# Differential attention: scores kept in SBUF by the maximum's pass, one exponential per map, values in two column tiles

## What is computed

```python
def one_block(qs):                     # a block of 128 queries, all heads
    a, b = qs
    p1 = softmax(einsum('bqhd,bkhd->bhqk', a, k1) * scale)
    p2 = softmax(einsum('bqhd,bkhd->bhqk', b, k2) * scale)
    return einsum('bhqk,bkhd->bqhd', p1 - lam * p2, v)
```

## Time and profile before

| | us |
|---|---|
| median of 3 runs (2815.12 to 2818.55) | 2816.46 |
| span of the profiled execution, first to last instruction | 2814.8 |
| PE busy in the span | 2441.5 (87%) |
| DVE busy | 2020.7 (72%) |
| ACT busy | 1417.5 (50%) |
| POOL busy | 760.7 (27%) |
| differential attention, about 475 to 818 us of the span | 343 |
| the exponential of 1024 scores, L588, 128 times | 143.5 |
| the maximum, L628, 128 times | 155.8 |

### The profile page before, as it was taken

How to read it: one execution, slowest core, us unless ns; L and a number is a source line. 1 busy time by engine, 2 the same in 40 slices (tenths; PEclk the granted TensorE clock), 3 DMA queues, 4 the chain that set the end, 5 groups by cost and what they waited for, 6 DMA issues and landing times. The chain is left out here.

```text
span 2814.8 us, 35573 instructions
## 1 busy us (share of the span) xinstructions
PE 2441.5 (87%) x10313; PEld 1685.3 (60%) x10314; DVE 2020.7 (72%) x2772; ACT 1417.5 (50%) x1999; POOL 760.7 (27%) x671
## 2 busy tenths in 40 slices
PE   7999598899989848989899989899999998988940
PEld 3555365444435537777678767677777776767730
DVE  1444355899955458887887888888888888888764
ACT  1121154787832146565654565655565565666530
POOL 1433200111101233333423242332242234343220
PEclk9999799899999879999999999999999999999975
DMA  4221542222105268695876687767676677788667
GB/s 180 64 64 50 126 86 74 45 47 61 31 19 97 68 232 307 227 314 201 303 253 211 225 294 245 261 234 255 240 285 228 218 273 281 253 284 309 209 220 272
DMA packets 383448, 538.20 MB, mean 191 GB/s; under 512 B 30008, under 2 KB 327488, under 8 KB 381328
## 3 DMA queue, kind: packets, MB, share of 16 engines
q1 hardware_dynamic: 358176, 498.21, 53.6%
q0 software_dynamic: 24048, 34.90, 3.3%
q10 hardware_dynamic: 1152, 4.19, 0.4%
HBM read 511.15 MB, written 60.15 MB: 203 GB/s over the span
## 5 line engine op out<-in xcount | busy, mean ns | idle before, releaser
L1611 DVE TENSOR_TENSOR wlo<-raw,whi 128x2048 fp32r<-128x2048 f32 x387 | 901.5, 2333 | 131.5 <-ACT whi L1544 90.3
L1544 ACT CAST whi<-raw 128x2048 fp32r<-128x2048 f32 x387 | 740.0, 1915 | 138.8 <-PE m_ps L1785 90.8
L1785 PE MATMUL m_ps<-whi,xt_hi 128*128 128x512 f32 x1056 | 442.0, 419 | 16.0 <-issue 15.4
L1785 PE MATMUL m_ps<-wlo,xt_hi 128*128 128x512 f32 x1056 | 430.0, 407 | 0.0
L1785 PE MATMUL m_ps<-whi,xt_lo 128*128 128x512 f32 x1056 | 428.6, 406 | 0.0
L1478 POOL TENSOR_SCALAR brow<-brow 1x1024 f32<-1x1024 f32 x33 | 101.3, 3070 | 673.0 <-issue 668.1
L410 PE MATMUL pp<-w_in_sb,ut 128*128 128x512 f32 (+3 forms) x688 | 271.1, 552 | 0.8 <-issue 0.8
L1785 PEld LDWEIGHTS m_ps<-whi,xt_hi 128*128 128x128 f32 x1056 | 210.4, 199 | 62.8 <-issue 15.8
L1785 PEld LDWEIGHTS m_ps<-whi,xt_lo 128*128 128x128 f32 x1056 | 209.1, 198 | 47.7
L1785 PEld LDWEIGHTS m_ps<-wlo,xt_hi 128*128 128x128 f32 x1056 | 210.2, 199 | 42.0
L1785 PE MATMUL y_ps<-whi,ht_hi 128*128 128x512 f32 x512 | 208.4, 407 | 0.0
(11 more groups left out here) (242 smaller groups left out, 4124.4 us busy)
## 6 DMA issues: line engine op xcount, KB each, us to landing
raw<-in_w_mlp SPq DMA_DIRECT2D x388, 1024.0 KB
yk<-y_dram SPq DMA_DIRECT2D x8, 2048.0 KB, 7.8
w_in_sb<-in_w_in SPq DMA_DIRECT2D x8, 1152.0 KB, 13.7
k_st<-qk_dram SPq DMA_DIRECT2D x32, 260.0 KB, 7.9
xs<-in_x SPq DMA_DIRECT2D x16, 512.0 KB, 7.7
q_st<-qk_dram SPq DMA_DIRECT2D x32, 256.0 KB, 7.0
qk_dram<-qk_hi SPq DMA_DIRECT2D x8, 832.0 KB, 4.5
qk_dram<-qk_lo SPq DMA_DIRECT2D x8, 832.0 KB, 7.5
```

The source lines that it names most:

```text
L1544: act.copy(whi[:, s, :, :], piece(k)).then_inc(hi_done, 1)
L1611: dve.tensor_tensor(wlo[:, s, :, :], piece(k), whi[:, s, :, :].bitcast(F32), ALU.subtract).then_inc(lo_done, 1)
L1785: ins = pe.matmul(bank, x[:, half, kc, :], w[:, s, i, :], start=(start and n == 1), stop=(stop and n == 3 * PK), skip_group_check=True)
```

## The change

`attend_diff` is rewritten in these parts; the shape of the pipeline, with 64 units and two maps, stays.

- The maximum's pass also writes the negated scores to SBUF, straight into `e`: `tensor_tensor_reduce` adds a tile of zeros, scales by -1 and takes the minimum starting from the negated meta maximum. The separate small combination goes. PE may overwrite `s_ps[i]` as soon as this pass is done.
- The meta scores are kept negated, and POOL copies a unit's 2 x 16 of them into the end of `e`. One exponential per map then reads all 1040 from `e` in place; its sum is the total. POOL's addition of partial sums goes.
- ACT does both exponentials of a step first and then the three copies of unit `n-2`, the meta part among them, which was DVE's.
- Values: chunks 4 to 7 write PSUM partitions 64 to 127, the others 0 to 63, in the order 0, 4, 1, 5, 2, 6, 8, 3, 7. The copy to `ot` has 128 partitions. The four transposes back become four products with `fold` (two identities on top of each other), which add the two halves.
- PE's order in a step becomes scores 0, values, scores 1, transposes, back, meta scores. Values lag seven steps, not six, and the meta scores of the next head come at `n % 8 == 5`, not 7.

```diff
+        zero = sb("zero", [P, SEQ])
+        fold = sb("fold", [P, DV])
-        STEPS = U + 8
+        LAG = 7
+        STEPS = U + LAG + 2
+        CHUNKS = (0, 4, 1, 5, 2, 6, 8, 3, 7)
+        weighed_in = lambda n: (n - LAG - 3) // 4 if n >= LAG + 3 and (n - LAG - 3) % 4 == 0 and (n - LAG - 3) // 4 < NG else None
+        back_in = lambda n: weighed_in(n - 1)
+        scores_in = lambda n: n // NT + 1 if n % NT == NT - 3 and n // NT + 1 < HD else None
...
         @block.scalar
+            def exponent(n, i):
+                act.wait_ge(nm_ready, 2 * n + i + 1)
+                act.wait_ge(meta_in, n + 1)
+                if n >= 16 and i == 0:
+                    act.wait_ge(ratio_done, n - 15)
+                k = (2 * n + i) % 4
+                act.activation(e[:, n % 2, i, :], e[:, n % 2, i, :], ACT.Exp, bias=nm[:, k:k + 1], scale=-1.0,
+                               accum_out=total[:, n % 16, i:i + 1]).then_inc(exp_done, 1)
...
+            def copy_meta(u):
+                act.wait_ge(x_ready, use_of[("meta", u)] + 1)
+                act.copy(pt[0:N_META, (u // 4) % 2, 8, (u % 4) * P:(u % 4 + 1) * P], x_ps[0:N_META, 0:P]
+                         ).then_inc(x_copied, 1)
...
             for n in range(STEPS):
+                if n < U:
+                    exponent(n, 0)
+                g = weighed_in(n)
                 if g is not None:
+                    act.wait_ge(o_ready, 2 * (g + 1))
                     if g >= 1:
                         act.wait_ge(x_ready, use_of[("back", g - 1)] + 1)
+                    act.copy(ot[:, :], o_ps[:, :]).then_inc(ot_done, 1)
+                if n < U:
+                    exponent(n, 1)
+                if 2 <= n <= U + 1:
+                    copy_first(n - 2)
+                    copy_second(n - 2)
+                    copy_meta(n - 2)
...
             def maximum(n, i):
+                k, at = (2 * n + i) % 4, 2 * (n % NT) + i
                 dve.wait_ge(scores_ready, 2 * n + i + 1)
                 if n % NT == 0 and i == 0:
+                    dve.wait_ge(x_copied, use_of[("scores", n // NT)] + 1)
                 if n >= 2:
                     dve.wait_ge(exp_done, 2 * n + i - 3)
+                    dve.wait_ge(combined, n - 1)
+                dve.tensor_tensor_reduce(e[:, n % 2, i, 0:SEQ], S(i), zero[:, :], -1.0, meta_nm[:, (n // NT) % 2, at:at + 1],
+                                         ALU.add, ALU.min, nm[:, k:k + 1]).then_inc(nm_ready, 1)
...
         @block.gpsimd
+                    pool.tensor_copy(e[:, n % 2, :, SEQ:KEYS], meta_s[:, h % 2, at:at + 2, :]).then_inc(meta_in, 1)
...
         @block.tensor
             def scores(n, i):
                 if n >= 1:
-                    pe.wait_ge(s_used, 2 * n + i - 1)
+                    pe.wait_ge(nm_ready, 2 * n + i - 1)
...
+            def transposes(u):
+                pe.wait_ge(combined, u + 1)
+                for g in range(2):
+                    if u >= 1:
+                        pe.wait_ge((first_copied, second_copied)[g], u)
+                    for c in range(4 * g, 4 * g + 4):
+                        ins = pe.transpose(t_ps[:, g, (c % 4) * P:(c % 4 + 1) * P], dsb[:, u % 2, c * P:(c + 1) * P], ident[:, :])
+                    ins.then_inc(t_ready, 1)
                 free_x(("meta", u))
                 pe.transpose(x_ps[0:N_META, 0:P], dsb[:, u % 2, SEQ:KEYS], ident[:, :]).then_inc(x_ready, 1)
...
                     vt = v_all[0:r, c, 128 + h * DV:128 + (h + 1) * DV]
-                    ins = pe.matmul(o_ps[0:DV, :], vt, pt[0:r, g % 2, c, :], start=(c == 0), stop=(c == 8))
+                    side = DV * (4 <= c < 8)
+                    ins = pe.matmul(o_ps[side:side + DV, :], vt, pt[0:r, g % 2, c, :], start=(c in (0, 4)), stop=(c in (3, 7)),
+                                    skip_group_check=True)
...
+            def back(g):
+                pe.wait_ge(ot_done, g + 1)
+                free_x(("back", g))
+                for j in range(4):
+                    ins = pe.matmul(x_ps[:, j * DV:(j + 1) * DV], ot[:, j * P:(j + 1) * P], fold[:, :],
+                                    start=True, stop=True)
+                ins.then_inc(x_ready, 1)
...
             for n in range(STEPS):
                 if n < U:
                     scores(n, 0)
+                if LAG <= n < U + LAG:
+                    q, i = divmod(n - LAG, 4)
+                    values(9 * q + 2 * i, 9 * q + 2 * i + (3 if i == 3 else 2))
                 if n < U:
                     scores(n, 1)
+                if 2 <= n <= U + 1:
+                    transposes(n - 2)
+                if back_in(n) is not None:
+                    back(back_in(n))
+                if scores_in(n) is not None:
+                    meta_scores(scores_in(n))
```

More of the change, by code:

```diff
@@ L556, in attend_diff @@
                 order.append(("back", back_in(n)))
-            if n % NT == NT - 1 and n + 1 < U:
-                order.append(("scores", (n + 1) // NT))
+            if scores_in(n) is not None:
+                order.append(("scores", scores_in(n)))
         use_of = {what: k for k, what in enumerate(order)}
@@ L608, in _ @@
                                          ALU.mult, ALU.add, lw[:, i:i + 1]).then_inc(lam_dots, 1)
+            dve.memset(zero[:, :], 0.0)
+            dve.tensor_tensor(fold[:, :], ident[:, 0:DV], ident[:, DV:P], ALU.add).then_inc(fold_set, 1)
             dve.wait_ge(lam_exp, 1)
@@ L651, in combine_halves @@
                                          in1=e[:, b, 0, :], op0=ALU.mult, op1=ALU.add).then_inc(combined, 1)
[L653 to L658, removed]
             def store_out(g):
@@ L683, in _ @@
                     store_out(back_in(n))
-                if n % NT == NT - 1 and n + 1 < U:
-                    meta_scores((n + 1) // NT)
+                if scores_in(n) is not None:
+                    meta_scores(scores_in(n))
         @block.gpsimd
@@ L689, in _ @@
             pool.wait_ge(lam_done, 1)
[L690 to L700, removed]
+            for n in range(U + 1):
+                if n < U:
+                    h, at = n // NT, 2 * (n % NT)
+                    if n >= 2:
+                        pool.wait_ge(combined, n - 1)
+                    pool.wait_ge(x_copied, use_of[("scores", h)] + 1)
+                    pool.tensor_copy(e[:, n % 2, :, SEQ:KEYS], meta_s[:, h % 2, at:at + 2, :]).then_inc(meta_in, 1)
+                if n >= 1:
+                    u = n - 1
+                    pool.wait_ge(inverted, u + 1)
+                    if u >= 2:
+                        pool.wait_ge(combined, u - 1)
+                    pool.tensor_scalar(ratio[:, u % 2:u % 2 + 1], total[:, u % 16, 0:1], inverse[:, u % 16, 1:2], lw[:, 5:6],
+                                       ALU.mult, ALU.mult).then_inc(ratio_done, 1)
         @block.tensor
@@ L771, in _ @@
                 if n < U:
                     scores(n, 1)
-                if weighing:
-                    values(m, m + 2)
-                g = back_in(n)
-                if g is not None:
-                    pe.wait_ge(ot_done, g + 1)
-                    free_x(("back", g))
-                    for j in range(4):
-                        ins = pe.transpose(x_ps[:, j * DV:(j + 1) * DV], ot[:, j * P:(j + 1) * P], ident[0:DV, 0:DV])
-                    ins.then_inc(x_ready, 1)
-                if n % NT == NT - 1 and n + 1 < U:
-                    meta_scores((n + 1) // NT)
+                if 2 <= n <= U + 1:
+                    transposes(n - 2)
```

103 lines of the change are left out of this document (29 added, 74 removed).

## The result

| | us |
|---|---|
| kernel before, median of 4 runs (2815.1 to 2820.6) | 2817.5 |
| changed kernel, median of 4 runs (3042.1 to 3051.0) | 3049.2 |
| ratio, 95% interval | 1.082 (1.081 to 1.084) |
| span of the profiled execution, before and after | 2814.8 and 3048.9 |

The direction was forecast, the size was not: +35 us forecast, +232 measured. Where the microseconds lie is read from two landmarks that both kernels have: the last `mixed` written from `x_ps` (the end of differential attention) and the 387 `wlo` of the experts.

The account below looks back on a forecast made before the run. VectorE was taken to set attention's pace, TensorE close behind. New TensorE waits gave +19 us at full clock, the lowered clock 16 more: +35 on 2814.8, so 2850; own range 2832 to 2880, overall 2805 to 2895.

Parts of the forecast that it names:

- The same times in every other stage: Outside differential attention, the experts included: a sign expected in the trace after, no change in time.
- The clock term: TensorE in differential attention: 21 idles of 3.3 us lower its clock, 0.8 us each, 16 us in all.
- rival D: Differential attention: TensorE's clock stays at its lower level through half the stage, +119 us, 2930; chance 0.06.
- the pair of chunks: TensorE's values in two column tiles: only three passes overlap, a pair 1.43 us, a step of three chunks 2.30.
- rival B: TensorE in attention: tiles overlap fully, a pair 1.00 us, and the clock stays up; +5, 2821 to 2826; chance 0.12.
- The wait: TensorE ahead of `back` and meta scores: idles 3.3 us, 21 times, until ScalarE has copied the meta part.
- The steps behind it: Attention steps after a TensorE wait: 7.46 us after `back`, 9.21 after meta scores, a head 43.8.
- Durations: Attention's instructions: pass 1.20 us, exponential 1.15, 16-row meta copy 0.26, fold products 0.93, plain steps 3.9 to 4.1.
- The faster rival: Differential attention: the waits for `x_ps` are covered and VectorE decides, 33.2 us a head, -50, 2767; chance 0.15.

Follow-up runs that it names:

- the filler run: Changed kernel with 64 increments, plus ten thrown-away score products in 20 of TensorE's 21 waits for the meta copy: 2839.5 us.
- the second order: Changed kernel with 64 increments; ScalarE's transpose copies before the exponentials, the `ot` copy before those, the meta copy before the second half's: 2784.7 us (0.987).
- the third order: On top of the second order, TensorE issues the next step's first scores ahead of the back or meta products: 2775.9 us (0.985).
- the tiles alone: Kernel before with only the values in two column tiles and the fold products, its own maximum, exponentials, copies and orders kept: 2828.0 us (1.003).

## Why the prediction was wrong, step by step

1. **"The same times in every other stage"** is the step that failed, by 166 to 173 us. The sum takes attention's difference for that of the whole kernel, which puts the experts at nothing without a reason: no stage but one was edited, and I took that for proof. But VectorE's program ahead of the experts' loop became shorter, and with that the loop moved across block boundaries. The q14 row of the kernel before (35 packets) shows that code is moved in pieces; where the loop lies is to be counted in the program, not read from this row.
2. **The clock term** was mis-sized: 21 x 0.8 = 16 us forecast, at least 44 measured (2883.5 - 2839.5). The earlier trace rows show one idle of 2.92 us, in the experts, and one microsecond of the some 3 at half clock after it. Here the clock stays at the half level after a meta wait from 700 to 714 us, 13 us, and after a `back` for some 3 us (720.2 to 723.3). The narrow meta products, which follow the wait at once, go with the long stretch; rival D had the right kind and too large a size. The excess of 28 us equals the miss in this stage, 62.7 measured and 35 forecast, but that is partly luck: the pair of chunks (point 4) was forecast too dear. By the prediction's own walk with the pair at 1.00 (rival B) the stage would cost 5 us more at full clock, and not 19, so the clock's part would be some 57 us, an estimate that the 44 of the filler run neither reaches nor excludes.
3. **The wait** was right in place, number, size and cause: 2.9 to 3.4 us, 21 times, forecast 3.3. The steps behind it were forecast too short by the clock: 8.6 us after most `back` (7.46 forecast), 13.4 after the meta scores (9.21), a head 51.1 (43.8). With the filler a head is 45.6.
4. **The pair of chunks** costs 1.00 us and not 1.43, three chunks 2.01 and not 2.30. TensorE's timeline at full clock:

```profile
724.77 1.08 PE L759 MATMUL o_ps<-pt,v_all 128*64 128x512 f32 x4
725.77 0.73 PE L715 MATMUL s_ps<-k_st,q_st 128*128 128x512 f32 x2
...
728.10 2.08 PE L759 MATMUL o_ps<-pt,v_all 16*64 16x512 f32 x6
730.11 0.73 PE L715 MATMUL s_ps<-k_st,q_st 128*128 128x512 f32 x2
```

   Rival B was right in this half, and with it the rule of the Trainium skill (TensorEngine Tiling (Array Packing), Key Properties) that tiles run side by side: 1.00 by it, 1.00 in the trace. My argument that in-order issue leaves only the middle passes to overlap was wrong.
5. **Durations** held within 7%. The pass took 1.28 us (1.20 forecast) and the exponential 1.16 (1.15):

```profile
L577 ACT ACTIVATE e<-e,nm 128x1040 f32<-128x1040 f32 x128 | 148.8, 1163 | 143.5 <-DVE nm L647 143.0
...
L647 DVE CUSTOM_DVE_ANT_0 e<-s_ps,zero,meta_nm 128x1024 f32<-128x1024 f32 x128 | 163.4, 1277 | 53.6 <-PE s_ps L715 46.9
```

   The next instruction starts 1.21 us after the pass (710.18 to 711.39), as worked out from the earlier trace rows; the meta copy takes 0.25 (0.26), the fold products 0.89 (0.93). Plain steps last 4.0 us.
6. **The faster rival** (2767 us) did not happen, but is near what the edit's parts can do: with the orders of ScalarE and TensorE mended 2775.9 was measured.

## What to carry to other kernels

An edit that adds or removes instructions ahead of a hardware loop can change the loop's time without touching it: count where the loop lies in each engine's program, compare the instruction queues' packets, and if it must touch a block more, move it with a few empty instructions. Price a new wait of TensorE by the work that then runs at the half clock, not by its own length, and fill it with work that is due anyway; and when an edit makes an engine lighter, first order the copies so that the one somebody waits for comes ahead of work that nobody needs yet.

## What the runs showed of the hardware

- A loop of 311 VectorE instructions, whose body stands three times behind conditions, stands still for 7.6 us in the mean in nearly every iteration when it touches three blocks of 256 (235.3 / 31) and hardly at all when it touches two (16.4 us in all). The time differs by 165 to 173 us, less than the 219 us of the gaps, so a part of them costs nothing.
- Two column tiles of 64 in plain f32 run wholly side by side: a pair of 512-column chunks in 1.00 us, the price of one.
- After a wait of 3.4 us followed by 16 narrow products TensorE ran at half clock for 13 us; after one of 0.44 us in the second order it still did, for some 6 us that hold three chunks of values (at 647.4 us of that trace). With the same products directly behind wide ones the clock stayed at 1.00 in the kernel before and in the third order, and fell for some 3 us with the tiles alone; what decides isn't settled.
